# A hybrid RWKV-7 and sparse-attention decoder step: shorter gap fillings, and three more pairs of weight tiles in each layer's dense stages

## What is computed

```
per layer:
  h = x @ w_in                      # one projection: r, k, v, w_lo, a_lo, z_A | q, 6 kv, gates, z_B | g_A, g_B
  o_A = GroupNorm(rwkv7_scan(r, decay, k, v, a, b, state)) + bonus, times silu(z_A)
        # prompt: scan over 256 tokens; samples: one step from the given states
  o_B = (compressed-block, selected-block and window attention of 16 heads, gated) * silu(z_B)
        # prompt: its own keys; samples: pages of a cache of 256 tokens
  m   = sigmoid(g_A) * (o_A @ w_up_a) + sigmoid(g_B) * (o_B @ w_up_b)
  x   = LayerNorm(ALPHA * x + m @ w_out)
returns y, the new kv rows, window rows, recurrence states and shift rows
```

## Time and profile before

| | |
|---|---|
| runs, us | 2149.66, 2151.95, 2152.32 (median 2151.95) |
| span of the profiled execution, us | 2147.6 (the page gives no other time of that execution) |
| PE, DVE, POOL, ACT busy | 98%, 51%, 24%, 19% |
| filling matmuls (L791) | 2816 records, 692.3 us, 395 ns each |
| chain that ended last | PE 96%, DVE 3%, DMA 1% |
| weight loads by SP | 512 KB each, median 3.8 to 4.6 us from issue to landing |

### The profile page before, as it was taken

How to read it: one execution, slowest core, us unless ns; L and a number is a source line. 1 busy time by engine, 2 the same in 40 slices (tenths; PEclk the granted TensorE clock), 3 DMA queues, 4 the chain that set the end, 5 groups by cost and what they waited for, 6 DMA issues and landing times.

```text
span 2147.6 us, 48884 instructions
## 1 busy us (share of the span) xinstructions
PE 2111.1 (98%) x21468; PEld 1863.6 (87%) x21468; DVE 1085.1 (51%) x1884; ACT 411.9 (19%) x1169; POOL 505.7 (24%) x377
## 2 busy tenths in 40 slices
PE   9999999999999999999999999999999999999997
PEld 8999977777887779999999999777777877899996
DVE  4554344443726524773666442545557165247745
ACT  1111111222103411110211111222221143111002
POOL 3433300002011123333233333000020112134331
PEclk9999999999999999999999999999999999999998
DMA  8545333335543365554455454232264434655551
GB/s 299 175 160 173 117 133 101 101 101 220 198 138 119 114 220 177 164 178 160 133 182 166 166 166 139 83 101 101 101 243 165 133 104 144 218 169 164 173 169 66
DMA packets 88981, 329.51 MB, mean 153 GB/s; under 512 B 11905, under 2 KB 11921, under 8 KB 86465
## 3 DMA queue, kind: packets, MB, share of 16 engines
q1 hardware_dynamic: 74592, 268.60, 37.3%
q0 software_dynamic: 11872, 53.59, 7.1%
q10 hardware_dynamic: 2304, 4.20, 0.6%
HBM read 315.91 MB, written 18.82 MB: 156 GB/s over the span
## 4 chain that ended last, share of the span: by engine, by line
PE 96%; DVE 3%; DMA 1%; issue 0%; ACT 0%; SPq 0%; DVEq 0%
PE PB L791 30%; PE PB L839 3%; PE PB L870 3%; PE PB L866 3%; PE PB L861 3%; PE PB L854 3%; PE PB L844 3%; PE PB L850 3%; PE PB L1274 3%; PE PB L771 1%; PE PB L926 1%; PE PB L1008 1%; PE PB L991 1%; PE PB L993 1%; PE PB L986 1%; PE PB L982 1%
## 5 line engine op out<-in xcount | busy, mean ns | idle before, releaser
L791 PE MATMUL PB<-XT,WT 128*128 128x264 f32 (+1 forms) x2816 | 692.3, 395 | 0.3 <-DMA WT<-in_w_all 0.2
L791 PEld LDWEIGHTS PB<-XT,WT 128*128 128x128 f32 (+1 forms) x2816 | 509.4, 189 | 101.1 <-issue 15.2
L1480 ACT ACTIVATE VT<-PB 128x132 f32<-128x132 f32 (+2 forms) x280 | 79.1, 291 | 578.9 <-PE PB L854 130.6
L1480 ACT ACTIVATE ARENA<-PB 128x128 f32<-128x128 f32 (+7 forms) x187 | 76.3, 429 | 262.1 <-PE PB L1173 65.7
L626 POOL DMA_DIRECT2D out<-in_c_win x16 | 8.1, 506 | 456.2 <-DVE ARENA L2094 456.2
L626 POOL DMA_DIRECT2D ARENA<-in_c_sel x64 | 40.0, 625 | 234.4 <-issue 234.4
L647 POOL TENSOR_TENSOR TOEP<-WT 128x1024 f32<-128x1024 f32 x20 | 47.2, 2358 | 170.5 <-PE PB L854 160.9
L647 POOL TENSOR_TENSOR TOEP<-H 128x1024 f32<-128x1024 f32 x20 | 48.2, 2410 | 143.7 <-PE PB L854 136.5
L850 PE MATMUL PB<-ARENA,TOEP 128*128 128x132 f32 x640 | 78.5, 276 | 0.0
L854 PE MATMUL PB<-ARENA,TOEP 128*128 128x132 f32 x640 | 78.5, 276 | 0.0
L861 PE MATMUL PB<-ARENA,TOEP 128*128 128x132 f32 x640 | 78.5, 276 | 0.0
(11 more groups left out here) (475 smaller groups left out, 4203.5 us busy)
## 6 DMA issues: line engine op xcount, KB each, us to landing
WT<-in_w_all SPq DMA_DIRECT2D x340, 512.0 KB, 4.4
H<-in_w_all SPq DMA_DIRECT2D x120, 512.0 KB, 4.6
KNVC<-in_w_all SPq DMA_DIRECT2D x40, 512.0 KB, 3.8
out<-in_c_win POOLq DMA_DIRECT2D x16, 512.0 KB, 5.2
ARENA<-in_c_cmp POOLq DMA_DIRECT2D x64, 128.0 KB, 4.4
ARENA<-in_c_sel POOLq DMA_DIRECT2D x64, 128.0 KB, 4.1
TOEP<-in_toep POOLq DMA_DIRECT2D x2, 2048.0 KB, 8.7
ARENA<-in_states POOLq DMA_DIRECT2D x4, 1024.0 KB, 11.4
```

Of the source, the lines that this page charges most:

```text
L791: ins = mm(PB[rows, bank, 0:T], WT[:, s, k, 0:rows.stop - rows.start], x, start=start, stop=stop)
L1480: return act(out, in_, ACT.Copy)
```

## The change

Kv tiles 8 and 9 go from the fillings to the main pairs (20 become 21 in each layer), ga tiles 4 to 7 go to the gate pairs (4 become 6); N_TILES falls from 46 to 40. The counts of the plan change at eight places: "bon" 4 to 3, "a1" 11 to 10, the last level's "y" 2 to 1 and "z" 4 to 3, the addition to "low" in round 0 from 9 to 6, "bc2" 5 to 3, "out1" 10 to 3, "pt1" 3 to 2 in each unit, "as1" 36 to 20, and "sc1" grows from 4 to 8. "mixers" no longer fills up to 20 tiles but by at most 7 matmuls. The other lines follow the indices.

```diff
@@ -68,18 +68,19 @@
 N_CONST = MASK_C + NB
 
 
-TILES = ([("lo", LO)] + [("kv", KV0 + i) for i in range(8, 12)] + [("gl", GL)] + [("q", Q0 + i) for i in range(8)]
-         + [("zb", ZB0 + i) for i in range(8)] + [("gb", i) for i in range(16)] + [("ga", i) for i in range(8)])
+LAST_GA = 4
+TILES = ([("lo", LO)] + [("kv", KV0 + i) for i in range(10, 12)] + [("gl", GL)] + [("q", Q0 + i) for i in range(8)]
+         + [("zb", ZB0 + i) for i in range(8)] + [("gb", i) for i in range(16)] + [("ga", i) for i in range(LAST_GA)])
 N_TILES = len(TILES)
 EARLY = 20
 MAIN = ([("v", V0 + i) for i in range(8)] + [("k", K0 + i) for i in range(8)] + [("r", R0 + i) for i in range(8)]
-        + [("z", Z0 + i) for i in range(8)] + [("kv", KV0 + i) for i in range(8)])
+        + [("z", Z0 + i) for i in range(8)] + [("kv", KV0 + i) for i in range(10)])
 MAINS = len(MAIN) // 2
 K_PAIR, R_PAIR, KV_PAIR = 4, 8, 16
 NORM_PAIR = 10
 LAST_ODD, EVENS = MAINS - 1 - MAINS % 2, (MAINS + 1) // 2
-PAIRED = [("ga", i) for i in range(8, 16)] + [("up", i // 2 + i % 2 * 8) for i in range(16)] + [("out", i) for i in range(16)]
-GATES, UPS, PAIRS = 4, 8, 8
+PAIRED = [("ga", i) for i in range(LAST_GA, 16)] + [("up", i // 2 + i % 2 * 8) for i in range(16)] + [("out", i) for i in range(16)]
+GATES, UPS, PAIRS = (16 - LAST_GA) // 2, 8, 8
 OUTS = GATES + UPS
 BOTH = OUTS + PAIRS
 HALF = T // 2
@@ -96,23 +97,23 @@
 GB_AT = [*range(V0, V0 + 9), KV0 + 6, KV0 + 7, KV0 + 10, KV0 + 11, GL, KV0, KV0 + 1]
 
 
-BEHIND = {"low": 16, "bon": 4, "a1": 11, "tok": 7}
+BEHIND = {"low": 16, "bon": 3, "a1": 10, "tok": 7}
 for level in range(1, LEVELS + 1):
-    BEHIND.update({f"y{level}": 1 if level < LEVELS else 2, f"z{level}": 2 if level < LEVELS else 4})
+    BEHIND.update({f"y{level}": 1, f"z{level}": 2 if level < LEVELS else 3})
 for chunk in range(NCH):
     BEHIND.update({f"r{chunk}": 1, f"u{chunk}": 1, f"s{chunk}": chunk // (NCH - 1)})
 
 
-BEHIND_MIX = {"v0": 4, "v1": 4, "v2": 4, "v3": 4, "vec": 101, "mu": 5, "mu2": 3, "sq": 0, "var": 10, "gbc": 5, "bc2": 5,
-              "h0": 12, "out0": 46, "h1": 12, "out1": 10}
-BEHIND_MIX.update({"cb": 12, "cbt": 3, "sc1": 4})
+BEHIND_MIX = {"v0": 4, "v1": 4, "v2": 4, "v3": 4, "vec": 101, "mu": 5, "mu2": 3, "sq": 0, "var": 10, "gbc": 5, "bc2": 3,
+              "h0": 12, "out0": 46, "h1": 12, "out1": 3}
+BEHIND_MIX.update({"cb": 12, "cbt": 3, "sc1": 8})
 for unit in range(UNITS):
     if unit + 2 < UNITS:
         BEHIND_MIX[f"sc{unit + 2}"] = 1
-    BEHIND_MIX.update({f"pt0{unit}": 3, f"pt1{unit}": 3, f"o{unit}": 0})
+    BEHIND_MIX.update({f"pt0{unit}": 3, f"pt1{unit}": 2, f"o{unit}": 0})
 
 BEHIND_MIX[f"o{UNITS - 1}"] = 12
-BEHIND_MIX.update({"as0": 12, "as1": 36, "as2": 6, "as3": 3})
+BEHIND_MIX.update({"as0": 12, "as1": 20, "as2": 6, "as3": 3})
 
 
 def plan():
@@ -124,8 +125,8 @@
         m = upto[L, "bc"] = m + 4
         for hq in range(NQUAD):
             for name, n in BEHIND.items():
-                m = upto[L, hq, name] = min(m + n + (0 if name != "low" else 9 if hq == 0 else 2 * L), first + EARLY * KT)
-        m = upto[L, "mixers"] = first + EARLY * KT
+                m = upto[L, hq, name] = min(m + n + (0 if name != "low" else 6 if hq == 0 else 2 * L), first + EARLY * KT)
+        m = upto[L, "mixers"] = min(m + 7, first + EARLY * KT)
         for name, n in BEHIND_MIX.items():
             m = upto[L, name] = min(m + n, first + N_TILES * KT)
         upto[L, "gates"] = first + N_TILES * KT
@@ -441,10 +442,10 @@
             if kind == "r":
                 eng.wait_ge(*step("mm_v", L * MAINS + R_PAIR + i // 2, "mix" + "ab"[i % 2]))
                 return
-            if kind == "kv" and i < 8:
+            if kind == "kv" and i < 10:
                 eng.wait_ge(*step("mp_a", L * MAINS + KV_PAIR + i // 2, "om"))
                 return
-            n = L * N_TILES + FIRST[kind] + (i - 8 if kind == "kv" else i)
+            n = L * N_TILES + FIRST[kind] + (i - 10 if kind == "kv" else i)
             eng.wait_ge(tile_out[n % 2], n // 2 + 1)
 
         def all_projected(eng, L, kind, i):
@@ -1432,7 +1433,7 @@
                     if g > 1:
                         pe.wait_ge(*step("up_v", L * UPS + g - 2, "fb"))
                     elif g:
-                        all_projected(pe, L, "ga", 7)
+                        all_projected(pe, L, "ga", LAST_GA - 1)
                     up_pair(L, g)
                 for j in range(PAIRS - 2):
                     out_pair(L, j, 0, UNITS_OF_PAIR)
@@ -1755,7 +1756,7 @@
                     sc.wait_ge(*step("gp_t", it, "st3"))
                     mark("gp_a", it, copy(FU[g % 2], first[:, 0:HALF]), "u")
                     sc.wait_ge(*step("gp_v", it, "fin"))
-                    gate = H[:, 8 + 2 * g:10 + 2 * g, :].rearrange("p t n -> p (t n)")
+                    gate = H[:, LAST_GA + 2 * g:LAST_GA + 2 + 2 * g, :].rearrange("p t n -> p (t n)")
                     mark("gp_a", it, act(gate, f, ACT.Tanh, scale=0.5), "tanh")
                 for g in range(UPS):
                     it = L * UPS + g
@@ -2441,7 +2442,7 @@
                         else:
                             fourth_sum(GATES + g + 1)
                     if g == 0:
-                        all_projected(ve, L, "ga", 7)
+                        all_projected(ve, L, "ga", LAST_GA - 1)
                         ve.wait_ge(*step("gp_a", (L + 1) * GATES - 1, "tanh"))
                     ga = H[:, g:g + 9:8, :]
                     gb = H[:, GB_AT[g]:GB_AT[g + 8] + 1:GB_AT[g + 8] - GB_AT[g], :]
```

## The result

The changed kernel takes **2176.0 us** (median of six runs, 2166.7 to 2181.7) against 2150.8 before (2145.9 to 2155.7). The ratio is 1.011 (95% interval 1.0093 to 1.0126), so it is slower by about 24 us. I had forecast slower by 11.6, at 2163.6, with bounds of 2156 and 2171: the right sign, half the size, outside the bounds. The profiled executions have spans of 2173.6 and 2147.6, 26.0 apart.

A forecast was written before the change was run, and what follows sets the result against it. TensorE, busy 98% of the span, was taken to bound the kernel. The terms -9.9 - 3.6 + 17.5 + 2.4 + 4.0 + 1.2 gave +11.6 us on the median 2151.95, so 2163.6 us, range 2156 to 2171.

The forecast's parts named there:

- Work saved: Six filling tiles per layer become three pairs; each pair saves 1.65 us, six save 9.9 us.
- gates: Remainder filling before the first gate pair, 49 matmuls cut to 9 and 3; PE stands for loads, 17.5 us over both layers.
- 2.4 of clock: One fall to 1.2 GHz behind each stand at the first gate pair, 1.2 us each, 2.4 us in all.
- mixers: Filling before the sample states' transposes; its cut lays bare 3.2 us in layer 0, 0.8 in layer 1: 4.0 us.
- sc1: Four added matmuls run in the 1.82 us stand for unit 0's product in each layer: -3.6 us.
- pt1: Attention units, one matmul cut in each; some 0.05 us lost in each of 16, 0.8 us.
- bon: Recurrence, layer 1: 0.38 us of slack against a cut of 0.445; 0.1 us in three rounds, 0.3 us.
- The cuts of low, a1, y5, z5, bc2, out1 and as1 stay inside their slack, so they cost nothing.: These fillings' cuts cost nothing, since DVE and ACT were done before PE came; all small cuts 1.2 us, 0 to 4.
- low: First "low" of layer 0 loses 3 matmuls; the cut stays inside its slack and costs nothing.
- The transfers land sooner: Rival: pair's blocks and sample states come early, "gates" stands 12.7 us, "mixers" costs nothing; 2154.8 us; chance 0.12.
- The clock falls for longer: Rival: falls twice as long at each stand, once more per layer by "out1" before the compressed scores; 2170.5 us; chance 0.12.

The follow-up runs named there:

- b_mix: Kernel before with "mixers" cut to 7 (8 matmuls fewer in layer 0, 2 in layer 1), which go to "gates"; ratio 1.0018, 3.9 us slower.
- a_as1: Changed kernel with "as1" 15 in place of 20, so 5 more matmuls stand in "gates" of each layer; ratio 1.0094 to the kernel before.
- b_low: Kernel before with "low" of round 0 alone cut by 3 matmuls, which go to "mixers"; ratio 1.0003.
- b_rec: Kernel before with only the recurrence's counts as in the change ("bon", "a1", last "y" and "z", "low"), 19 matmuls per layer to "mixers"; ratio 1.0047, again 1.0037.
- one_pair: Kernel before with only kv 8 and 9 paired, "sc1" 8, "as1" 20, other counts as before; ratio 0.9955, 2139.6 against 2148.7 us.
- b_a1: Kernel before with "bon" 3 and "a1" 10 alone, 8 matmuls per layer going to "mixers"; ratio 1.0035.
- b_rec_shift8: Kernel before with the recurrence's counts as in the change and 32 records added at the very start; ratio 1.0087, 19 us slower.

## Why the prediction was right in sign and wrong in size

- **Work saved, -9.9.** Right: products of 1.80 us, no stand between pairs from the second on.
- **"gates", 17.5 plus 2.4 of clock.** Right in sum. The two stages lost 8.4 and 11.8 us beyond the exchange of tiles, 20.2 against 19.9. Its parts were not quite so, and that they cancel is luck: the pair starts with its first block (5.99 and 8.59, less than 7.2 and 9.9), then DVE's s2 and s4, which I had left out, hold its fifth product, and the half clock costs 1.1 us, not 2.4, since most of it hides behind them. The first blocks took 4.24 and 4.16 us to land, near the 4.3 of the rows; the estimate of 3.2 us set beside it was too short.
- **"mixers", 4.0.** Right: b_mix cost 3.9. (By the plan it had 15 and 9 matmuls, not 16 and 10; 8 and 2 go either way.) In the changed kernel the stands are 3.00 and 0.63, and in layer 0 PE stood 1.05 us for a tile's load ahead of it too; what I had left out is the half clock behind (579), 1.7 us.
- **"sc1", -3.6.** Right: -4.0 alone.
- **"pt1" and "bon".** Right in size: a unit of the attention takes 7.78 us, before 8.15, so about 0.07 us of the 0.445 is lost in each; "bon" waits 0.05 us in each of three rounds.
- **"The cuts of low, a1, y5, z5, bc2, out1 and as1 stay inside their slack, so they cost nothing."** This is the step that failed. For y5, z5, "low" and "out1" it held in kernels of their own, for "as1" in the stages and in a_as1. But I asked only whether the releasing engine was done, and PE has one supplier more, as I read the stands, its code. In the kernel before, the cuts in "bon" and "a1" cost 7.5 us, all counts of the recurrence 8 to 10, up to 19 where the code lies worse. In the changed kernel's two profiles the rounds took 7.6 and 7.4 us more than forecast, 1.7 of it by the next point. The bounds allowed 4 for all small cuts.
- **"low".** In layer 1 PE waits 1.34 us for L2011 and then 0.35 for L2024. That is not in b_low or b_rec: with kv 8 and 9 gone, tile "gl" comes two tiles earlier and falls into this filling, and its matmuls, on half the columns, are shorter: the 22 of this filling take 7.9 us, where 22 plain ones take 9.8. I had priced a filling by its count. one_pair, with the same "gl" and the old count, has 0.5 us of this wait. The weights of "gl" in the changed kernel, and the wait in one_pair:
```profile
1372.28 1.98 PEld L792 LDWEIGHTS PB<-XT,WT 128*64 128x64 f32 x20 [0.34 <-issue]
```
```profile
PE PB L1084 <- DVE ARENA L2011: 0.5, 1, 0.5
```
- **The bounds.** The lower one, 2156, puts "gates" at 14.2 where the term's own lower bound was 12.7; with that it is 2154.4. The miss was at the other end.
- **The rivals.** "The transfers land sooner" failed (first block 4.2 us, "gates" and "mixers" far over 14.2 together). "The clock falls for longer" came nearest in time, but its mechanism did not hold: not at the gate pairs, not by "out1", but in the recurrence behind stands for code, and behind the sample states.

Added up: 11.6 + 8 to 10 (the counts of the recurrence alone) + 1.7 ("low") = 21 to 23, against 24. The changed kernel's own profile splits it otherwise: 11.6 + 5.9 (code, with the half clock behind it) + 1.7 ("low") = 19 of 26, and most of the rest is the half clock in layer 0. What is left open: why "bon" and "a1" count and y5 and z5 don't, and when a stand of 1.3 to 2.5 us brings the clock down (that of 1.73 at 1459.8 did, that of 2.21 in b_a1 did not). That it is the fetch rests on the numbers modulo 256, the packets ahead of the stands and their moving with the code. No run took the fetch itself away, and none put the old counts of the recurrence back into the changed kernel; one_pair, which has them, comes nearest.

## What to carry to other kernels

Before a filling is shortened, name every supplier of the engine behind it: the engines it waits for, the transfers further on, and its own code where it issues many small instructions. Price a filling by what it covers and by the time of its own matmuls, not by their number. And where a remainder is filled at the end of a plan, look there first: here the largest cost came from a line that the diff does not touch, and one_pair, which leaves it long enough and keeps the counts of the recurrence, is faster than both kernels. A stretch without any wait for an engine can still have no slack.

## What the runs showed of the hardware that I had not expected

As I read them, PE's stands for code end only at every 256th of its records, nearly always 2.2 to 2.5 us after a 16 KB packet of the instruction queue began (up to 3.8), and they cost up to 2.5 us each in a stretch of small matmuls. Most boundaries are passed without a stand: 73 stands of 0.3 us or more in 3380 boundaries. Moving the code by 32 records changes which of them are held: with the same counts the kernel went from 1.0047 and 1.0037 to 1.0087, while the kernel before did not slow down by it. Of the 30 stands for code of 1.27 to 2.54 us in the traces, 16 were followed within 2.5 us by 1.2 GHz, for 3 to 20 us, and that can cost more than the stands: 17 us against 7.9 in b_rec_shift8. Ahead of the first gate pair, where the next blocks and sums were still to come, the half clock cost 0.1 and 1.0 us.
